# Low halves of the ga and gb weight slabs by accumulating transfers instead of VectorE, and gb in three passes

## The reference, cut to what matters

```
h = x @ w_in + b_in
conv_a, conv_g, q, k, v, r, f_lr, gate_a, gate_b = split(h)
y_conv = conv_module(conv_a, conv_g, ...)          # 31-tap convolution, layer norm, silu, matmul
y_gla  = gla_branch(q, k, v, r, f_lr, ...)         # gated linear attention, matmul
merged = sigmoid(gate_a) * y_conv + sigmoid(gate_b) * y_gla
mix    = merged @ w_out + b_out
x      = layer_norm(1.19 * x + mix)
x      = layer_norm(1.19 * x + hier_moe(x))        # 64 experts, two of them per token
```

## Time and profile before

| | |
|---|---|
| median of three runs | 1691.71 us |
| profiled execution, its own time | 1691.89 us |
| its span | 1689.8 us, so 2.1 us lie around it |
| busy: TensorE, VectorE, ScalarE, GpSimd | 1364.6, 674.2, 472.0, 59.0 us |
| mean granted clock of TensorE | 0.914 |

### The profile page before, as it was taken

How to read it: one execution, slowest core, us unless ns; L and a number is a source line. 1 busy time by engine, 2 the same in 40 slices (tenths; PEclk the granted TensorE clock), 3 DMA queues, 4 the chain that set the end, 5 groups by cost and what they waited for, 6 DMA issues and landing times.

```text
span 1689.8 us, 21326 instructions
## 1 busy us (share of the span) xinstructions
PE 1364.6 (81%) x8600; PEld 883.5 (52%) x8600; DVE 674.2 (40%) x1109; ACT 472.0 (28%) x682; POOL 59.0 (3%) x27
## 2 busy tenths in 40 slices
PE   8999999976656666665666667566799999999998
PEld 7789988522212212221221222122499999778887
DVE  5787979311101100110111011001367888655874
ACT  4454233401001001010010010010265764546653
POOL 0000000670000000000000000000000000000000
PEclk9999999988787978887888888788999999999999
DMA  9433555899999999999999999999944325474440
GB/s 359 156 138 138 218 204 245 353 431 430 432 431 431 431 433 433 431 431 432 433 433 431 431 432 433 431 432 431 419 165 150 139 71 197 167 258 175 179 174 25
DMA packets 50441, 530.79 MB, mean 314 GB/s; under 512 B 4276, under 2 KB 5556, under 8 KB 33862
## 3 DMA queue, kind: packets, MB, share of 16 engines
q1 hardware_dynamic: 50374, 529.86, 75.8%
HBM read 528.80 MB, written 1.05 MB: 314 GB/s over the span
## 4 chain that ended last, share of the span: by engine, by line
PE 51%; DMA 39%; DVE 6%; ACT 3%; issue 1%; SPq 0%; DVEq 0%; ACTq 0%
DMA shared<-in_w 37%; PE psum L454 6%; PE psum L456 6%; PE psum L455 6%; PE psum L1433 6%; PE psum L367 5%; PE psum L2222 4%; PE psum L1456 4%; PE psum L2223 2%; PE psum L1462 2%; PE psum L1404 2%; PE psum L2059 1%; DVE ring_parts L590 1%; DMA arena<-in_w 1%; PE psum L611 1%
## 5 line engine op out<-in xcount | busy, mean ns | idle before, releaser
L1433 PE MATMUL psum<-ring,arena 128*32 128x512 f32 x992 | 145.3, 739 | 86.8 <-DMA ring<-in_w 86.6
L1433 PE MATMUL psum<-shared,arena 128*32 128x512 f32 x1040 | 151.0, 726 | 61.5 <-DMA shared<-in_w 61.4
L1665 DVE TENSOR_TENSOR shared<-shared,psum 128x512 f32<-128x512 f32 x16 | 11.0, 688 | 462.3 <-PE psum L1433 462.3
L1456 PE MATMUL psum<-shared 128*32 128x512 f32 x512 | 89.5, 834 | 68.4 <-DMA shared<-in_w 68.4
L454 PE MATMUL psum<-parts 128*128 128x256 f32 (+1 forms) x424 | 136.5, 322 | 0.7 <-DVE parts L532 0.7
L455 PE MATMUL psum<-parts 128*128 128x256 f32 (+1 forms) x424 | 135.1, 319 | 0.0
L1433 PEld LDWEIGHTS psum<-ring,arena 128*32 128x32 f32 x992 | 34.3, 132 | 185.3 <-DMA ring<-in_w 100.2
L456 PE MATMUL psum<-parts,ring_parts 128*128 128x256 f32 x464 | 131.2, 283 | 0.0
L1433 PEld LDWEIGHTS psum<-shared,arena 128*32 128x32 f32 x1040 | 38.2, 129 | 168.3 <-issue 91.8
L456 PE MATMUL psum<-parts 128*128 128x256 f32 (+1 forms) x392 | 126.1, 322 | 0.0
L454 PE MATMUL psum<-parts,ring_parts 128*128 128x256 f32 x400 | 114.8, 287 | 0.4 <-ACT shared L2256 0.4
(11 more groups left out here) (343 smaller groups left out, 2347.4 us busy)
## 6 DMA issues: line engine op xcount, KB each, us to landing
shared<-in_w SPq DMA_DIRECT2D x47, 4096.0 KB, 32.4
ring<-in_w SPq DMA_DIRECT2D x47, 4096.0 KB, 32.4
ring<-in_w_in SPq DMA_DIRECT2D x19, 2048.0 KB, 8.7
ring<-in_w_ffn_gate_up SPq DMA_DIRECT2D x11, 2048.0 KB, 8.2
ring<-in_w_gate SPq DMA_DIRECT2D x8, 2048.0 KB, 7.9
ring<-in_w_ffn_down SPq DMA_DIRECT2D x5, 2048.0 KB, 7.8
ring<-in_w_out SPq DMA_DIRECT2D x4, 2048.0 KB, 8.6
shared<-in_w SPq DMA_DIRECT2D x6, 1024.0 KB, 28.8
```

What stands on the lines that cost most here:

```text
L1433: m = pe.matmul(ps[slots, bank, :], V.picked[:, k, slots], w[e * len(w) // QUAD][:, e % (QUAD // len(w)), j, :], start=(k == 0), stop=(k = ...
L1456: m = pe.matmul(ps[slots, MOE_BANK["down"][c], :], V.hidden_t[:, f, slots], w(e), start=(f == 0), stop=(f == ET - 1))
```

## The change

The slabs `gb0` and `gb1` join the list of those that are cut, as units 44 to 51. From unit 36 on (`BY_DMA`) the low part is made another way. ScalarE writes minus the high part into the buffer of the low part (one more copy, scale -1, semaphore `in_minus`), then the high part. GpSimd waits for `in_minus` and issues a transfer of the same 128x1024 weights from HBM (`w_in_units`, a second copy of these four slabs in the order of units) that adds them to what stands in the buffer. TensorE waits for the high copy and for this transfer. These units have four buffers instead of three, one of them in the place of `v`, so the first of them waits until the last `kv` matmul has read it. A load into a ring slot of these slabs waits for ScalarE's copy instead of for `in_low`. VectorE's loop has no low parts from unit 36 on and puts more taps into the turns there. `moe_read0` is raised after `gb1`. Some semaphores are shared (`piece_in`, `router_exp`) with counts moved accordingly.

```diff
-    SLABS = [..., "r0", "r1", "ga0", "ga1"]
+    SLABS = [..., "r0", "r1", "ga0", "ga1", "gb0", "gb1"]
-    BUFS = 3
+    BUFS, WIDE = 3, 4
+    BY_DMA = 4 * SLABS.index("ga0")
...
+        slot = 12 + n % self.BUFS if n < self.BY_DMA else (6, 12, 13, 14)[(n - self.BY_DMA) % self.WIDE]
+        return self.K.parts(slot, 1024, 1024 * low).rearrange("p (k n) -> p k n", k=k)
+
+    def before(self, n):
+        if n == self.BY_DMA:
+            return None
+        return n - (self.WIDE if n > self.BY_DMA else self.BUFS)
...
     def high(self, L, n):
         src = self.source(L.eng, n)
-        if n >= self.BUFS:
-            self.wait_read(L.eng, n - self.BUFS)
+        if n == self.BY_DMA:
+            self.K.banks1.wait_full(L.eng, f"kv{NC - 1}_1")
+        elif n >= self.BUFS:
+            self.wait_read(L.eng, self.before(n))
+        if n >= self.BY_DMA:
+            L.done(L.eng.activation(self.part(n, 1), src, ACT.Copy, scale=-1.0), self.K.sem("in_minus"))
         L.done(L.eng.activation(self.part(n, 0), src, ACT.Copy), self.K.sem("in_high"))
+
+    def low_by_dma(self, pool, n):
+        m = n - self.BY_DMA
+        pool.wait_ge(self.K.sem("in_minus"), m + 1)
+        pool.dma_start(self.part(n, 1).rearrange("p k n -> p (k n)"), self.K.d["w_in_units"][m], accum_op=ALU.add)\
+            .then_inc(self.K.sem(f"low_added{m % self.WIDE}"), 16)
...
     def wait_low(self, eng, n):
-        eng.wait_ge(self.K.sem("in_low"), n + 1)
+        m = n - self.BY_DMA
+        if m < 0:
+            eng.wait_ge(self.K.sem("in_low"), n + 1)
+        else:
+            eng.wait_ge(self.K.sem("in_high"), n + 1)
+            eng.wait_ge(self.K.sem(f"low_added{m % self.WIDE}"), 16 * (m // self.WIDE + 1))
...
     slab_tiles("ga1", "ga", 4)
+    for s in range(2):
+        slab_tiles(f"gb{s}", "gb", 4 * s)
     pe.drain().then_inc(S("moe_read0"), FREED)
-
-    for s in range(2):
-        pe_slab_tiles(K, pe, B, R, f"gb{s}", tiles("gb", 4 * s, 4), x)
...
-    for n in range(split.units):
-        split.low(L, n)
+    for n in range(split.BY_DMA + 8):
+        if n < split.BY_DMA:
+            split.low(L, n)
         done = n - split.BUFS
-        pace = 0 if done < 0 else 2 if done < 4 or 8 <= done < 12 else 4
+        pace = 0 if done < 0 else 2 if done < 4 or 8 <= done < 12 else 4 if n < split.BY_DMA else 7
...
-            pace = 1
+            pace = 4
...
         if before in InSplit.SLABS:
-            split.wait_low(sp, split.unit(before) + 3)
+            last = split.unit(before) + 3
+            if last < split.BY_DMA:
+                split.wait_low(sp, last)
+            else:
+                sp.wait_ge(S("in_high"), last + 1)
...
+def block1_pool(K, pool):
+    split = InSplit(K)
+    for n in range(split.BY_DMA, split.units):
+        split.low_by_dma(pool, n)
```

More of the change, by code:

```diff
@@ L348, in rstd, with first_slab_at @@
         return self.A(2, T, 1024 if i == 3 else 240 + T * i)
+    def first_slab_at(self, slot):
+        return self.ring_cols(slot * SLOT_COLS, SLOT_COLS).rearrange("p (m k n) -> p m k n", m=4, k=DT)
     def first_slab(self, ring):
-        return self.ring_cols(ring.slot("a0") * SLOT_COLS, SLOT_COLS).rearrange("p (m k n) -> p m k n", m=4, k=DT)
+        return self.first_slab_at(ring.slot("a0"))
     def slab(self, slot, k=DT):
@@ L486 @@
 class InSplit:
-    SLABS = ["g0", "a1", "g1", "k", "v0", "v1", "q", "r0", "r1", "ga0", "ga1"]
+    SLABS = ["g0", "a1", "g1", "k", "v0", "v1", "q", "r0", "r1", "ga0", "ga1", "gb0", "gb1"]
     ROWS = ("k", "v0", "v1")
-    BUFS = 3
+    BUFS, WIDE = 3, 4
+    BY_DMA = 4 * SLABS.index("ga0")
     def __init__(self, K):
@@ L503, in part @@
         k = 2 if self.SLABS[n // 4] in self.ROWS else DT
-        return self.K.parts(12 + n % self.BUFS, 1024, 1024 * low).rearrange("p (k n) -> p k n", k=k)
+        slot = 12 + n % self.BUFS if n < self.BY_DMA else (6, 12, 13, 14)[(n - self.BY_DMA) % self.WIDE]
[4 more added lines that the diff above has]
+        return n - (self.WIDE if n > self.BY_DMA else self.BUFS)
     def source(self, eng, n):
         slab, i = self.SLABS[n // 4], n % 4
-        w = self.K.slab(self.K.ring1.wait_landed(eng, slab))
+        slot = self.K.ring1.wait_landed(eng, slab)
+        if n >= self.BY_DMA:
+            return self.K.first_slab_at(slot)[:, i]
+        w = self.K.slab(slot)
         return w[:, 2 * i:2 * i + 2, :] if slab in self.ROWS else w[:, :, i * P:(i + 1) * P]
@@ L736, in block1_pe @@
         b = B.take(pe, f"co{n}")
-        pe.wait_ge(S("in_low"), end.FIRST + n + 1)
+        pe.wait_ge(S("in_low"), end.FIRST_LOW + n + 1)
         w = end.part(n, 0), end.part(n, 1)
@@ L876, in outputs @@
             evac(f"ga{m}", K.tiles(8, DT)[:, m, :], ACT.Sigmoid, bias=K.v("b_ga", m))
+        elif slab in ("gb0", "gb1"):
+            m = i + 4 * int(slab[2])
+            evac(f"gb{m}", K.tiles(9, DT)[:, m, :], ACT.Sigmoid, bias=K.v("b_gb", m))
     kdec, o = K.tiles(10, TT, GDK, TT * GDK), K.tiles(4, DT)
@@ L1221, in load_first @@
     def load_first(m):
-        sp.dma_start(first[:, m].rearrange("p k n -> p (k n)"), d["w_in_first"][m]).then_inc(S(f"first_in{m}"), 16)
+        sp.dma_start(first[:, m].rearrange("p k n -> p (k n)"), d["w_in_first"][m]).then_inc(S(f"piece_in{m}"), 16)
     def load_x(half):
@@ L1504, in moe_act @@
         L.done(act.activation(W.gexp[:, t, :], W.logits[:, t, 0:NG], ACT.Exp, bias=W.group_max[:, t:t + 1],
[L1505 removed]
+                              accum_out=W.gsum[:, t:t + 1]), S("router_exp"))
     act.wait_ge(S("expert_below"), 1)
     for t in range(TT):
[L1508 removed]
+        L.done(act.activation(W.eexp[:, t, :], W.masked[:, t, :], ACT.Exp, bias=W.expert_max[:, t:t + 1]), S("router_exp"))
     for t in range(TT):
         L.done(act.activation(W.top2_exp[:, t, :], W.top8[:, t, 0:2], ACT.Exp, bias=W.expert_max[:, t:t + 1],
[L1511 removed]
+                              accum_out=W.sums[:, t:t + 1]), S("router_exp"))
     act.preload_act_table(ACT.Sqrt)
@@ L1757, in moe_load @@
             for piece in (1, 2, 3):
-                sp.sem_inc(S(f"w2_piece{piece}"), 16)
+                sp.sem_inc(S(f"piece_in{piece}"), 16)
         return
@@ L1761, in moe_load @@
         h = slice(SLAB_COLS // 4 * piece, SLAB_COLS // 4 * piece + SLAB_COLS // 4)
-        sp.dma_start(dst[:, :, h], src[:, :, h]).then_inc(S(f"w2_piece{piece}") if piece else ring.landed(t), 16)
+        sp.dma_start(dst[:, :, h], src[:, :, h]).then_inc(S(f"piece_in{piece}") if piece else ring.landed(t), 16)
 def moe_load_extra(K, sp, n):
@@ L2947, in host_arrays @@
     out["w_in"] = np.stack([by_partition(w[:, IN_COLS[n]:IN_COLS[n] + 512]) for n in IN_SLABS])
+    units = [np.stack([by_partition(w[:, IN_COLS[n] + m * P:IN_COLS[n] + (m + 1) * P]) for m in range(4)])
+             for n in ("ga0", "ga1", "gb0", "gb1")]
+    for n, u in zip(("ga0", "ga1", "gb0", "gb1"), units):
+        out["w_in"][IN_SLABS.index(n)] = u.transpose(1, 0, 2).reshape(P, SLOT_COLS)
+    out["w_in_units"] = np.concatenate(units)
     out["w_in_first"] = np.stack([by_partition(w[:, O_A + m * P:O_A + (m + 1) * P]) for m in range(4)])
@@ L2963, in host_arrays @@
     return {n: np.ascontiguousarray(v) for n, v in out.items()}
-INPUTS = ("x", "x_rows", "mem", "vecs", "rows", "gains", "consts", "consts2", "w_router", "w_in", "w_in_first", "w_in_f", "w_conv_out", "w_gate_up", "w_gla_out",
+INPUTS = ("x", "x_rows", "mem", "vecs", "rows", "gains", "consts", "consts2", "w_router", "w_in", "w_in_units", "w_in_first", "w_in_f", "w_conv_out", "w_gate_up", "w_gla_out",
           "w_out", "w1", "w3", "w2", "w_in_2", "w_rows_2", "w_gate_2", "w_branch_2", "w_out_2", "pool_w_2", "w_mem_kv_2",
```

17 lines of the change are left out of this document (8 added, 9 removed).

## The result

The changed kernel takes 1702.48 us, the median of four runs (1701.29 to 1705.29); the kernel before took 1691.72 (four runs, 1690.87 to 1692.46) beside it. The ratio is 1.0066 with a 95% interval of 1.0054 to 1.0079: slower by 10.8 us, where 2 us faster was forecast. The time lies outside the range.

What follows compares the result with a forecast made beforehand. TensorE alone was taken to bound 144 to 240 us, block 1's gain moving the end equally; 1691.9 - 4.6 (gb in three passes) + 2.2 (late transfers) = 1689.5 us, range 1686.8 to 1694.0.

Steps and rivals of the forecast that it cites:

- the share of the overload: Units 43 to 51: of 10 us too much DMA work, loads bear half or more, TensorE 5 us at most.
- The single collision: A unit sharing the engines with a load takes 5.7 + 2.7 = 8.4 us, 1.4 us too late.
- the prediction's first case: Accumulate's second read is free: nine units cost the DMA engines 12 us, all 29 in 31; only single units late.
- The stall taken, 2.2 us: TensorE's loss to late units: one full collision with go1 (1.4 us), one of 0.8 with mem and the gain.
- rival 2: Four buffers turn too slowly at units from 40 on; at 10.5 us per landing stalls are 10.6, time 1697.9; chance 0.20.
- The loads counted: 17 us of SyncE's transfers beside units 43 to 51: go1 5.4, mem, gain and router's weights 6.2, co0 5.4.
- Three passes: gb on TensorE: eight results at 2.87 instead of 3.45 us, 4.6 us less on the path.
- Landing alone: GpSimd's accumulating 512 KB transfer, undisturbed: 4.9 us as a plain 1 MB transfer plus 0.8 for issuing, 5.7 us.
- The price on the engines: DMA engine time per unit: 1.35 us if the accumulate's second read is free, 2.7 if not.
- 8.7 us before: Stretch before the expert phase's transfer at 303.8: DMA busy 0.59, so block 1's gain or loss moves the end equally.
- Rival 1: No unit's transfer is late, the second read is free and queues give way: 1687.3 us; chance 0.34.
- Rival 3: ScalarE at 3.1 us a unit costs 2.8 us (1690.1), or VectorE's taps still end at 224 (1690.6); chance 0.08.

Runs made afterwards that it cites:

- both slabs in pieces: Changed kernel with go1 and co0 each loaded as four transfers of 1024 columns (4 KB packets instead of 16): 1697.53 us, ratio 1.0029.

## Why the prediction was wrong

**The step that failed** is the share of the overload. The prediction had the right figures for the doubled price, "41 us in 31", and went on: "10 us too much must be borne; nothing waits for co0, mem or go1 before 207, so they bear half or more, and 5 us at most fall on TensorE." Lateness is not divided up in that way. When full engines serve a load and a unit in turns, each is late by work of the other: go1 took 4.3 us longer, mem 13, and TensorE lost 13.5 us all the same. The single collision was also mis-sized: a unit was to be late by its own work (5.7 + 2.7 = 8.4 us, 1.4 too late), while it waits for much or all of the load's (9.7 to 11.9 us beside one 2 MB load). And the overload is not needed for it: plain copies, the prediction's first case with "12" us for nine units, in which only single units were to be late by next to nothing, cost 7.0 us of stalls.

**The stall taken, 2.2 us,** measured 13.5. Of these about 8.0 are idle time behind unit 42 and 3.7 slow clock behind the long stalls; 1.8 I did not separate. The prediction named the slow clock, but with rival 2 only, and put no price on it in its own sum. (The row it read there shows the slow clock behind small matmuls, with no idle time before it; that idle times come before it too, only the runs after show.) With the measured 2.95 us for a unit the overload is 9 x 2.95 + 17 - 31 = 12.6 us, and 8.0 to 9.8 of it fell on TensorE: most of it, where the prediction had half at most.

**The loads counted** also came at other times, go1 at 177 and co0 at 193.4 where 174 and 186 were expected, and they left out go0, which is in flight when unit 40's transfer is issued (9.89 us in the chain of waits). Of the 3.0 us lost before unit 42, unit 40 bears 1.3; the rest is not settled, since the versions with late loads have between 1.5 and 2.7 us there too (unit 42 at 182.39 and 183.54), that without transfers 0.6 (181.51).

**What held.** Three passes: 4.6 us forecast; 5.1 by the pace of the changed kernel, and a last gb result 5.0 us earlier where nothing is transferred. Landing alone: 5.7 forecast, 5.5 measured, in part by luck: the 0.8 us for GpSimd's issuing were those of another kind of instruction, and it measured 0.86. The price on the engines: 2.7 or 1.35 us, and it was the first, 2.95. ScalarE hides its copies. The taps' end: 207 forecast, 211.6 measured, 4.6 us later since the head norms came later (176.4, not 172), with 82 taps in just the 32.5 us computed. The stretch behind gb kept its length within 0.5 us, though the "8.7 us before" that it was read from end at 298.7, 5.1 us ahead of the issue at 303.8, and the DMA share in between was 0.81.

**The rivals.** Rival 1 (no unit late, 1687.3) is near what the kernel does without transfers, 1688.95 (3.6 us under the kernel before, not 4.6). Rival 2 (1697.9) had the right sign; its price was the way through GpSimd, which is 5.5 us when alone. Its turning point of 8.5 us was passed (8.7 at the median) because of the loads, and the loss sits in a few stalls, not in each unit. Rival 3 didn't come.

## What to carry to other kernels

Before work is moved from an engine to a transfer, add up the busy time of the 16 DMA engines over the stretch, the moved transfer at its price beside the loads that are there; an accumulating transfer counts about twice. If the sum exceeds the stretch, the engine that waits for the transfer pays most of the excess, whatever else is late, and the clock's loss behind long stalls with it. Even if the sum fits, look at each meeting by itself: a 512 KB transfer that met a 2 MB load landed 4 to 6 us later, nearly as long as the load keeps the engines busy, and whatever the wait has to spare must cover that. Then look which loads are not needed yet: issuing them behind the last of the urgent transfers was worth 13 us here.

## What the runs showed of the hardware

- An accumulating transfer of 512 KB from HBM into the on-chip buffer keeps the 16 engines for 2.95 us (2.77 in the changed kernel), a plain one for 1.59; alone they land in 5.5 and, at the shortest, 3.7 us. Beside a 2 MB load of SyncE's the units got 44% of the engines' time and moved 0.70 MB in 8 us; without it 1.47. GpSimd spends 0.86 us on issuing the first kind, 0.53 on the second.
- TensorE's granted clock in the 4 us behind idle times: 0.57 behind 1.8 us of idle time and 0.50 behind 3.5 us in the changed kernel, 0.50 behind 5.0 us with go1 late; but 1.00 behind 1.7 us with both slabs in pieces.
- A subtraction of 128x1024 numbers on GpSimd takes 2.5 us. A tap of VectorE's that meets one takes 2.6 us, otherwise 0.48 (0.40 from one to the next).
